# Projections and prompt attention inside the first fused block, shortest tiles first; delta norms chunk by chunk; output projection re-paced

## The reference

```python
h = x + 0.5 * rms_norm(swiglu_ffn(rms_norm(x, norms[0]), f1_gu, f1_d), norms[1])
mix = token_mixer(rms_norm(h, norms[2]), ...)
h = h + rms_norm(mix, norms[3])
h = h + 0.5 * rms_norm(swiglu_ffn(rms_norm(h, norms[4]), f2_gu, f2_d), norms[5])

def token_mixer(u, ...):
    proj = u @ w_in
    qkv_dn, z, a, b, q_sb, k_sb, v_sb = jnp.split(proj, cuts, axis=-1)      # 1536, 512, 4, 4, 512, 512, 512 columns
    qkv_dn, new_conv = causal_short_conv(qkv_dn, conv_hist, conv_w)         # 4 taps, then SiLU
    q_dn = l2_normalize(...) * (DN_K_DIM ** -0.5); k_dn = l2_normalize(...)
    o_dn, s_new = gated_delta_rule(q_dn, k_dn, v_dn, g, beta, s0)           # 4 heads of 128
    o_dn = rms_norm(o_dn, dn_norm) * jax.nn.silu(z)
    o_sb = rms_norm(stick_breaking_attention(q_sb, k_all, v_all, ...), sb_norm)  # 8 heads of 64
    return concatenate([o_dn, o_sb]) @ w_o, k_sb, v_sb, s_new, new_conv

# stick breaking, for one block of 128 queries against the keys s < t:
z = (q.k / sqrt(d)) + bias
a[t,s] = sigmoid(z_ts) * prod_{s<j<t} (1 - sigmoid(z_tj));   o = a @ v
```

## Time and profile before

| | before |
|---|---|
| median of 3 runs | 3040.1 us (3038.89 to 3040.31) |
| the profiled execution, its own time | 3044.16 us, span 3042.4 us |
| mean granted clock of PE | 0.929 of full speed |
| busy PE, DVE, ACT, POOL | 88%, 41%, 26%, 10% of the span |
| memory traffic | 223 MB, mean 73 GB/s |

### The profile page before, as it was taken

How to read it: one execution, slowest core, us unless ns; L and a number is a source line. 1 busy time by engine, 2 the same in 40 slices (tenths; PEclk the granted TensorE clock), 3 DMA queues, 4 the chain that set the end, 5 groups by cost and what they waited for, 6 DMA issues and landing times. The chain is left out here.

```text
span 3042.4 us, 40856 instructions
## 1 busy us (share of the span) xinstructions
PE 2675.9 (88%) x16736; PEld 2391.2 (79%) x16736; DVE 1253.7 (41%) x1786; ACT 793.3 (26%) x1369; POOL 301.5 (10%) x232
## 2 busy tenths in 40 slices
PE   7999999999869999456547999976889999999997
PEld 7999999999759999333336887754679999999996
DVE  4333333333555310266654554325533333333334
ACT  4111111111333322345433443303431111111112
POOL 0000000000201100123330213200100000000002
PEclk9999999999979999677768999967989999999999
DMA  4211111111222321100035447514212111111112
GB/s 139 70 42 55 41 41 41 41 41 41 90 61 89 95 71 50 51 1 1 0 136 168 151 147 234 176 48 158 79 64 70 42 55 41 41 41 41 41 48 92
DMA packets 130348, 223.26 MB, mean 73 GB/s; under 512 B 9765, under 2 KB 74277, under 8 KB 130236
## 3 DMA queue, kind: packets, MB, share of 16 engines
q1 hardware_dynamic: 125964, 208.55, 20.7%
q0 software_dynamic: 4272, 13.15, 1.5%
HBM read 193.18 MB, written 28.48 MB: 73 GB/s over the span
## 5 line engine op out<-in xcount | busy, mean ns | idle before, releaser
L974 PE MATMUL pr_pm<-u_uh,pr_w_hi 128*128 128x352 f32 x672 | 221.5, 330 | 0.6 <-ACT pr_hist L1045 0.6
L976 PE MATMUL pr_pm<-u_uh,pr_w_lo 128*128 128x352 f32 x672 | 216.7, 322 | 0.0
L975 PE MATMUL pr_pm<-u_ul,pr_w_hi 128*128 128x352 f32 x672 | 216.5, 322 | 0.0
L325 DVE TENSOR_TENSOR y_y<-y_y,a_q 128x512 f32<-128x512 f32 x180 | 123.4, 686 | 190.8 <-PE a_q L249 190.8
L325 DVE TENSOR_TENSOR x_mixed<-x_mixed,c_q 128x512 f32<-128x512 f32 x180 | 123.0, 687 | 190.8 <-PE c_q L249 190.8
L162 PE MATMUL a_q<-u_uh,a_hi_g 128*128 128x352 f32 x528 | 171.7, 325 | 1.4 <-DVE u_ul L408 1.4
L162 PE MATMUL c_q<-c_uh,c_hi_g 128*128 128x352 f32 x528 | 171.4, 325 | 1.4 <-DVE c_ul L408 1.4
L162 PE MATMUL c_q<-c_uh,c_hi_u 128*128 128x352 f32 x528 | 170.6, 323 | 0.0
L162 PE MATMUL a_q<-u_uh,a_hi_u 128*128 128x352 f32 x528 | 170.6, 323 | 0.0
L163 PE MATMUL a_q<-u_ul,a_hi_g 128*128 128x352 f32 x528 | 170.2, 322 | 0.0
L164 PE MATMUL a_q<-u_uh,a_lo_g 128*128 128x352 f32 x528 | 170.0, 322 | 0.0
(11 more groups left out here) (440 smaller groups left out, 5955.9 us busy)
## 6 DMA issues: line engine op xcount, KB each, us to landing
b_page<-in_cache_k SPq DMA_DIRECT2D x128, 256.0 KB, 3.4
b_page<-in_cache_v SPq DMA_DIRECT2D x128, 256.0 KB, 3.6
pr_raw<-in_w_in SPq DMA_DIRECT2D x14, 1024.0 KB, 5.4
a_raw_g<-in_ffn_gu SPq DMA_DIRECT2D x11, 1024.0 KB, 5.1
a_raw_u<-in_ffn_gu SPq DMA_DIRECT2D x11, 1024.0 KB
a_raw_d<-in_ffn_d SPq DMA_DIRECT2D x11, 1024.0 KB
c_raw_g<-in_ffn_gu SPq DMA_DIRECT2D x11, 1024.0 KB, 5.1
c_raw_u<-in_ffn_gu SPq DMA_DIRECT2D x11, 1024.0 KB
```

Source lines behind the costliest of these rows:

```text
L325: nc.vector.tensor_tensor(part, part, self.pd[n % 2], ALU.add).then_inc(self.E("added"), 1)
L974: nc.tensor.matmul(pm[e][t][:, 0:TB], wh, uh[:, c, cols], start=(c == 0), stop=False)
L975: nc.tensor.matmul(pm[e][t][:, 0:TB], wh, ul[:, c, cols], start=False, stop=False)
L976: last = nc.tensor.matmul(pm[e][t][:, 0:TB], wl, uh[:, c, cols], start=False, stop=(c == KC - 1))
```

## The change

- The blocks `projections` and `prompt_attention` are gone. Their work stands in two classes, `Project` and `Attend`, whose streams are woven into `first_half`'s last part on each engine. The order of the units is query, key and value of pair 0 and of pair 1, six convolution units, pair 2, two convolution units, pair 3, four convolution units, four gate units. The first four units (`EARLY`) are projected bank by bank while the last down halves and the turning of `uh` still run.
- A unit has two PSUM banks in place of six: each bank waits for the evacuation of the bank two before. Attention has two banks for scores (512 keys of two heads), two for the transposes, one for the rest.
- The eight tiles of a pair run shortest first, with two `ex` buffers in place of four, and one `wt`. The results go to DRAM (`o_rows`, 2 MB) and come back to `mixed` in the delta block.
- Rows are stored from SP's queue, not POOL's. SiLU (16 times) runs in place, followed each time by a load of the table set with exp and ln.
- In the delta block the norms are made chunk by chunk, 11.5 steps ahead of each chunk, without Sqrt and without the six loads. The gates stand earlier.
- In `second_half` the times of the streams change, as well as in the last down halves (`down_last`, `add_last`) and at the input's norm.

```diff
 def down_last(self, pe):
     for n in range(2 * (NT + 1)):
-        yield n // 2 + 0.5 * (n % 2)
+        yield 1.4 * n
@@ add_last
-        yield n // 2 + 0.5 * (n % 2) + 0.5
+        yield 1.4 * n + 1.6
...
+EARLY = 4
+def piece_time(n, t):
+    return (25.5, 44.0, 62.0)[t] + 3.9 * n if n < EARLY else 77.5 + 16.5 * (n - EARLY) + 5.5 * t
...
+class Project:
+    def multiply(self, pe, split):
+        order = sorted((piece(n, t), n, t) for n in range(N_UNITS) for t in range(3))
+        for at, n, t in order:
+            yield piece_time(n, t)
+            if n < EARLY and n == 0:
+                pe.wait_ge(split, 2 * (3 * t + 3))
+            if t == 0:
+                pe.wait_ge(E("rest"), n + 1)
+            at_least(pe, E("evac"), at - 1)
+            for c in range(KC):
+                (three matmuls into self.pm[at % 2])
...
+    def activate(self, act):
+        for n in SILU_UNITS:
+            yield unit_end(n) + (7.0 if kind == "conv" else 1.0)
+            if kind == "conv":
+                act.wait_ge(E("tapped"), 8 * c + 8)
+            nc.scalar.activation(self.post_of(n)[:], self.post_of(n)[:], ACT.Silu).then_inc(E("silu_done"), 1)
+            nc.scalar.preload_act_table_set("natural_log_exp_and_others")
...
+class Attend:
+    PAIR = 96.0
+    START = 81.0
+    TILES = list(range(NT))
+    def time(self, m, offset):
+        hp, i = self.tile(m)
+        begun = sum(j + 1 for j in self.TILES[0:m % NT])
+        return self.START + self.PAIR * (hp + begun / 36) + offset * max((i + 1) / 8, 0.3)
...
+    def weigh(self, pool):
+            yield self.time(m, 17.0)
+            pool.wait_ge(self.E("decayed"), m + 1)
+            self.nc.gpsimd.tensor_tensor(x, x, self.run[m % 2][:, :, 0:self.keys(m)], ALU.mult)
+    def turn(self, pe):
+                yield self.time(m, 21.7 + n)
+                if n == 0:
+                    pe.wait_ge(E("weighted"), m + 1)
+                at_least(pe, E(f"copied{at % 2}"), at // 2)
+    def sums(self, pe):
+            yield self.time(m, 26.4)
+            for z in range(2):
+                pe.wait_ge(E(f"copied{z}"), self.pieces[m + 1] // 2)
+            at_least(pe, E("o_done"), m)
+            ...
+            yield self.time(m, 28.5)
+            pe.wait_ge(E("ot_copied"), m + 1)
...
@@ first_half, tensor
-            interleave(f.down_last(pe), turn2.pe(pe))
+            interleave(f.down_last(pe), turn2.pe(pe), project.multiply(pe, turn2.lo_half), attend.scores(pe), attend.turn(pe), attend.sums(pe),
+                       project.turn_rows(pe), project.multiply_ab(pe))
@@ first_half, vector
-                    yield turn1.times[i] - 0.6
+                    yield (-3.6, -3.5, -2.3)[i] if i < 3 else turn1.times[i] - 0.6
-                        yield -2.3 + 0.5 * e + 0.1 * (k == "u")
+                        yield (-0.95, 1.05)[e] + 0.1 * (k == "u")
@@ second_half
 turn_mixed
-                    yield i - 1.2
+                    yield i - 0.55
 finish
-                    yield i - 2.5
+                    yield i - 1.55
 norms_mid
-                    yield i + 1.1
+                    yield i + 1.3
-                    yield i + 1.5
+                    yield i + 1.9
 norms_out
-                    yield i + 1.9
+                    yield 2.8 * i + 6.2
@@ delta_and_sample
+        def norm_time(i):
+            return begin(i) - 11.5 if i < NT else begin(2) - 6.0
 gates (PE)
-                yield -13.0
+                yield -15.5
-                nc.scalar.activation(norm[:], norm[:], ACT.Sqrt).then_inc(E("norm_root"), 1)
-                nc.scalar.preload_act_table_set("natural_log_exp_and_others")
+                    nc.scalar.activation(rn[:, i, :], norm[:, i, :], ACT.Ln).then_inc(E("norm_log"), 1)
+                    nc.scalar.activation(rn[:, i, :], rn[:, i, :], ACT.Exp, scale=-0.5).then_inc(E("norm_root"), 1)
```

More of the change, by code:

```diff
@@ L409, in dve @@
                                              self.uh[:, c, cols].bitcast(F32), ALU.subtract).then_inc(self.lo_half, 1)
-def first_half(nc, x, norms, ffn_gu, ffn_d, h1, uh, ul, y, ident):
+XP = T_P + 3 + N_B * (L_S + 3)
+TAIL = 3 * (1 + N_B)
+AB0 = QKV + DN
+BIG = 2.0 ** 40
+UNITS = ([("query", 0), ("key", 0), ("value", 0), ("query", 1), ("key", 1), ("value", 1)] + [("conv", c) for c in range(6)]
+         + [("query", 2), ("key", 2), ("value", 2), ("conv", 6), ("conv", 7), ("query", 3), ("key", 3), ("value", 3)]
+         + [("conv", c) for c in range(8, 12)] + [("gate", c) for c in range(4)])
@@ new lines, with unit_of, unit_column @@
+N_UNITS = len(UNITS)
+EARLY = 4
+ROW_UNITS = [n for n, (kind, c) in enumerate(UNITS) if kind != "query"]
+NAT_UNITS = [n for n in ROW_UNITS if UNITS[n][0] != "value"]
+POST_UNITS = [n for n, (kind, c) in enumerate(UNITS) if kind in ("conv", "gate", "value")]
+SILU_UNITS = [n for n, (kind, c) in enumerate(UNITS) if kind in ("conv", "gate")]
+def unit_of(kind, c):
+    return UNITS.index((kind, c))
+def unit_column(kind, c):
+    return {"conv": 0, "gate": QKV, "query": AB0 + 8, "key": AB0 + 8 + SB, "value": AB0 + 8 + 2 * SB}[kind] + P * c
@@ L1476, in delta_and_sample @@
         o_rows = s.sb("o_rows", [P, G, SB])
+        stage = o_rows
         abx = s.sb("abx", [P, NT + 1, 8])
@@ L1939, in weights @@
                 nc.scalar.activation(mixed[0:T_S, NT, DN:D], pm[0:T_S, :], ACT.Copy).then_inc(E("gathered_out"), 1)
-            interleave(chain(), advance(), gates(), prepare(), key_copies(), weigh(), weights())
+            interleave(chain(), advance(), gates(), norms(), prepare(), key_copies(), weigh(), weights())
         @block.vector
@@ L1978, in gates @@
                 then(nc.vector.memset(norm[:, NT, :], 1.0))
-                for i in range(NT + 1):
-                    yield K0 - 1 + 0.45 * i + 0.04
-                    rows_n = P if i < NT else T_S
-                    dve.wait_ge(E("squared"), i + 1)
-                    nc.vector.tensor_reduce(norm[0:rows_n, i, :], squares(i).rearrange("p (h c) -> p h c", c=P), AX.X, ALU.add).then_inc(E("reduced"), 1)
-                yield -13.5
+                yield -15.8
                 dve.wait_ge(E("delta_masks"), 1)
@@ L2123, in _ @@
             dve.wait_ge(E("zeros_made"), 1)
-            interleave(chain(), advance(), gates(), prepare(), key_copies(), logits(), weigh(), keep())
+            interleave(chain(), advance(), gates(), norms(), prepare(), key_copies(), logits(), weigh(), keep())
 def delta_sample(nc, g, big_g, last_decay_s, fac, qkv_nat, tri_s, level_s, spread_s, ident, states, mixed, states_out):
```

1081 lines of the change are left out of this document (547 added, 534 removed).

## The result

The changed kernel takes 2928.7 us (median of 4 runs, 2925.5 to 2933.9) against 3040.2 us (4 runs); the ratio of the runs is 0.9633, 95% interval 0.9614 to 0.9652. It is 111.5 us faster. Forecast were 2880 us and a range of 2795 to 2970: the side was right and the time lies in the range, but outside the 2840 to 2915 us that the likeliest case had for itself. The gain was 160 us in the forecast and 112 in the run.

What follows compares the result with a forecast made beforehand. The prediction took TensorE to bound the projections and chain latency the prompt attention, one behind the other. -112 - 25 - 12 - 7 - 5 = -161 us from 3044.2 gave 2883, at the median 2879, rounded to 2880; range 2795 to 2970 us.

Steps and rivals of the forecast that it cites:

- the likeliest case: Whole kernel: projections and attention fill each other and the seams go; 2880 us, own range 2840 to 2915, chance 0.48.
- The merged part: Projections woven with prompt attention, early part included: 93 + 546 + 12 = 651 us against 763, so -112 us.
- the two short waits: Merged part, each tile: TensorE waits 0.7 us before its sums and 0.5 before the transpose back; 32 tiles, 38 us.
- the delta block's 92%: TensorE's busy share in the delta block's middle, taken for the merged streams: 467 us of work becomes 508 us.
- Rival "TensorE nearly full": Merged part: slack in every chain step lets both streams fill each other, total -236, 2804 us; chance 0.17.
- Rival "ports and bad overlap": Merged part: VectorE and POOL block each other (2965 us) or the two stages overlap badly (2945 us); chance 0.22.
- The signs: Profile after: delta block from near 1440 us, TensorE 84 to 90% busy, clock 0.95 or more, output projection some 150 us.
- Rival "the queues walk the chain": Merged part: shared engine queues delay evacuations and stop TensorE; no overlap gives 3241 us, deciding from 177 us a pair; chance 0.10.
- The delta block's opening: Delta block's start: the first chunk needs only its own rows' norms, so waiting falls; -25 us, bounds -10 and -36.
- Output projection: Its loop through the gate's load, 15.3 us a tile, shortens; half of 23 us, -12 us, bounds 0 and -23.
- Tail: Final norms: VectorE's own work bounds a tile, about 2.7 us in place of 3.62; -7 us, bounds 0 and -8.
- Start: Kernel's start: third tile's norm goes ahead of weight splits, so the first feed-forward matmul comes earlier; -5 us, bounds 0, -8.

Runs made afterwards that it cites:

- rows_late_spread: The changed kernel with the convolution units' row transposes 4 to 8 us later in the order; 2923.3 us.
- stretched_long: The changed kernel with tiles longest first, convolution row transposes 4 to 8 us later, and a tile's chain steps 1.25 times farther apart; 2870.6 us.
- st14_sep: As st14, with the sums 0.8 and the transpose back 1.7 steps later; 2843.6 us.
- second_old: The changed kernel with the output projection's and the tail's order as before the change; 2951.1 us.
- st14: As stretched_long, with a tile's chain steps 1.4 times farther apart in place of 1.25; 2870.2 us.
- tail_no_add: The changed kernel with the last residual's add on POOL left out but for 8 columns; 2919.0 us.
- start_old: The changed kernel with the first norms, turns and weight splits in the order of before; 2932.9 us.

## Why the prediction was right, and where its sum was off

- *The merged part, -112, measured -52.* The mechanism of the likeliest case was the right one: the seams are gone, TensorE is the engine to fill, clamps and ports matter little. Its size was not. The mis-sized term is the share that the streams fill: 86% of the main part forecast, 80% measured, at clock 0.91 where the sum had taken the full clock. In us: 121 idle for 79 + 12, and busy 490 for 467. Of the idle time, the term of 38 us for the two short waits was not too small (17 in the change, 29 with the "issue" time). Too small was what the delta block's 92% allowed for all other waits, 41 us and 12 for the end: it was 92 us, most of it before the row transposes (56) and before the attention's transposes (25). Both are places where lateness shows and not where it comes from, as rows_late_spread shows; what brings it out is the distance between the steps in the written order. stretched_long and st14_sep, the same work with other constants and the tiles longest first, take 554 and 528 us in place of 611. Why the delta block fills to 92% and this part does not is not shown by any run. Of the busy time, st14_sep needs 458 us for the same matmuls at clock 0.97, so the count of 467 was not too low. Busy time times granted clock, an estimate of the work at full clock, is 446 us in the change and 444 in st14_sep; by it the count was some 20 us too high and the clock's price in the change nearer 44 us than 23.
- *Rival "TensorE nearly full", 2804.* Not reached; st14_sep, at 87% busy, is 40 us above it.
- *Rival "ports and bad overlap", 2945 to 2965.* The time, 2928.7 us, lies 16 us from it and 49 from the forecast; the wide range held because it took this rival in. The half about overlap is right in kind, though less bad than one stage after the other. The half about ports is wrong in size for the merged part: no clamp is blocked, and three taps and one split cost VectorE 6 us. What else the lock did is in the tail.
- *The signs.* Of those that the forecast named, the gates' matmuls (19.8 us after the block's start), the output projection (132.8 us, shorter than the 150) and the idle time before sums and transposes back (29 us for 32 tiles) came as said. The delta block's first instruction at 1495.7 us for 1440, TensorE's 80% for 84 to 90, the clock of 0.91 for 0.95 and the rounds of the tail did not.
- *Rival "the queues walk the chain".* The mechanism of a queue that stands for another stream's wait is real (1303 to 1315 us), its price is a third of what would decide: (611 - 12)/4 = 150 us a pair against 177.
- *The delta block's opening, -25, measured -34.* The gates' matmuls came 60.4 us after the block's start, now 19.8; the first chunk's chain (L1705 and its new line L1788) 102.8, now 64.8:

```profile
1515.49 0.38 PE L1733 MATMUL b_D<-m_g,m_masks 128*128 128x32 f32 x2 [0.18 <-DVE b_gm L2070]
...
1560.55 0.60 PE L1788 MATMUL b_D<-w_ident,b_xt 128*128 128x128 f32 x4
```

  That is 38 us, beyond my bound of 36, and the chunks give 4 back (from the chain's start in the first chunk to that in the last it is 297.7 us before, 302.1 after). No run here takes the norms apart from the rest, so this is read from the traces and not shown by an edit.
- *Output projection, -12, measured -26 (23 in the trace of second_old).* I had taken half of 23 us; the whole of it came, and a little more, since a tile takes 11.8 us of TensorE and not the 12.4 of my count. The gate's load was the loop.
- *Tail, -7, measured -2.* POOL's add and the final norm exclude each other, which the step "VectorE's own work bounds it" left out; I had applied that rule to the attention and not here, where its two conditions (two inputs of VectorE in SBUF, and a GpSimd instruction that reads SBUF) stand in the code. In second_old, with the old order and the same adds, every norm takes 1.28 us and the round is 3.62.
- *Start, -5, measured -6* in the trace, and 1 to 4 us by the edit, which is within what can be told.

Two small gains larger than forecast (by 9 and 14 us) covered a part of the 60 us that the merged part fell short. That is luck: the misses had different causes and went opposite ways. Without them the program would have taken some 2952 us, an estimate from these two numbers.

## What to carry to other kernels

Where streams of several engines are woven by written times, the distance between a step and the one that it waits for is a quantity to tune by itself: find TensorE's waits, and before moving the one that shows, ask whether the wait only moves on, as late rows did; spreading the whole chain gave 39 us and separating two neighbouring steps 27 where moving one gave 5, which is no difference. Look at TensorE's busy time and granted clock along with its idle time: in the change, stretched_long and st14_sep idle times of 121, 81 and 70 us came with 490, 473 and 458 us busy at clocks of 0.91, 0.96 and 0.97 for the same matmuls. It is no fixed rate, since in rows_late_spread 11 us less of idle time came with 8 us more of busy time. And look for every pair of a GpSimd operation and a VectorE operation with both inputs in SBUF, also in a tail that seems a plain chain: there the two durations add up, here to 3.6 us a tile.

## What the runs showed that I had not expected

Taking out the SiLU made the kernel slower, because loads of exp's and ln's tables came in its place (65 for 45). In going from st14 to st14_sep 12 us less of idle time came with 13 us less of busy time for the same matmuls, at a granted clock of 0.95 and then 0.97. And the merged part varies more from run to run than the delta block. In the four traces whose merged part is the same (the change, tail_no_add, second_old, start_old) it is 1474.7 to 1482.3 us from the first feed-forward matmul to the delta block's first table load, and 486.6 to 488.5 from there to the first turning. A difference of a few us between two merged parts, each read from one trace, is therefore not safe.
